# Twenty-four gate products of a merge as pairs by seven half-size products, with the sums of their weights made in DRAM

## What is computed

```python
gates = jax.nn.sigmoid(p["gate"] + merge_gate_b).reshape(Bn, S, N_BRANCH, D_MODEL)
merged = (gates[:, :, 0] * y_ml + gates[:, :, 1] * y_gla
          + gates[:, :, 2] * y_conf + gates[:, :, 3] * y_sc)
return merged @ w_o
```

## Time and profile before

| what | value |
| --- | --- |
| median of 3 runs | 1973.35 us (1972.5 to 1974.92) |
| the profiled execution | 1973.15 us, span 1971.2 us |
| granted PE clock, mean | 0.999 of full speed |
| PE, DVE, ACT, POOL busy | 1959.5, 1291.6, 893.8, 128.4 us |
| merge loop, one output tile | 27.2 us |

### The profile page before, as it was taken

One profiled execution on the slowest core, in us unless ns is written; L12 is line 12 of the kernel. 1 busy time (PEld: TensorE's weight loads), 2 busy tenths in 40 slices (PEclk: granted clock), 3 DMA queues, 4 the chain that ended last, 5 costly groups with the idle time before them and its releaser, 6 DMA issues.

```text
span 1971.2 us, 29262 instructions
## 1 busy us (share of the span) xinstructions
PE 1959.5 (99%) x10404; PEld 1640.5 (83%) x10404; DVE 1291.6 (66%) x2073; ACT 893.8 (45%) x1417; POOL 128.4 (7%) x202
## 2 busy tenths in 40 slices
PE   9999999999999999999999999999999999999999
PEld 7777789898987888898998888778888888888888
DVE  6555578676687776787786679484444786653545
ACT  4555555445444554544454443564333544432333
POOL 0111011111111111000001000000000000000000
PEclk9999999999999999999999999999999999999999
DMA  5899968677666115666656313111322412232222
GB/s 200 211 232 240 203 180 204 198 188 189 221 209 150 55 50 149 199 177 186 191 178 244 110 44 106 64 65 66 106 96 96 144 43 86 95 100 103 93 93 91
DMA packets 92909, 278.80 MB, mean 141 GB/s; under 512 B 10488, under 2 KB 13560, under 8 KB 92560
## 3 DMA queue, kind: packets, MB, share of 16 engines
q1 hardware_dynamic: 67200, 187.20, 29.1%
q0 software_dynamic: 24896, 88.14, 18.8%
q10 hardware_dynamic: 720, 2.23, 0.3%
HBM read 275.39 MB, written 52.47 MB: 166 GB/s over the span
## 4 chain that ended last, share of the span: by engine, by line
PE 95%; DVE 2%; DMA 1%; ACT 1%; issue 0%; SPq 0%; DVEq 0%; ACTq 0%
PE bank L962 23%; PE bank L964 23%; PE bank L963 23%; PE bank L1285 4%; PE bank L1287 4%; PE bank L1286 4%; PE bank L1085 1%; DMA w_raw<-in_wstream 1%; PE bank L1144 1%; PE bank L1067 1%; PE bank L1160 1%; PE bank L1070 1%; PE bank L1018 1%; PE bank L1112 1%; PE bank L1020 1%; PE bank L1019 1%
## 5 line engine op out<-in xcount | busy, mean ns | idle before, releaser
L962 PE MATMUL bank<-b_hi,w_hi 128*128 128x512 f32 x2060 | 812.3, 394 | 2.7 <-DVE w_lo L3172 1.3
L964 PE MATMUL bank<-b_hi,w_lo 128*128 128x512 f32 x2060 | 802.2, 389 | 0.0
L963 PE MATMUL bank<-b_lo,w_hi 128*128 128x512 f32 x2060 | 802.0, 389 | 0.0
L962 PEld LDWEIGHTS bank<-b_hi,w_hi 128*128 128x128 f32 x2060 | 386.8, 188 | 91.1 <-issue 8.4
L964 PEld LDWEIGHTS bank<-b_hi,w_lo 128*128 128x128 f32 x2060 | 386.8, 188 | 81.1
L963 PEld LDWEIGHTS bank<-b_lo,w_hi 128*128 128x128 f32 x2060 | 387.0, 188 | 80.2 <-issue 2.4
L2835 DVE TENSOR_TENSOR w_lo<-w_raw,w_hi 128x1024 fp32r<-128x1024 f32 (+3 forms) x259 | 306.7, 1184 | 216.9 <-ACT w_hi L1879 216.0
L1879 ACT ACTIVATE w_hi<-w_raw 128x1024 fp32r<-128x1024 f32 (+3 forms) x259 | 265.6, 1025 | 285.0 <-PE bank L964 265.6
L3995 DVE SCALAR_TENSOR_TENSOR arena<-bank,vec,arena 128x511 f32<-128x511 f32 x88 | 65.7, 749 | 85.9 <-ACT arena L2729 80.6
L1285 PE MATMUL bank<-parts,w_hi 128*128 128x256 f32 x384 | 108.1, 282 | 0.1
L1287 PE MATMUL bank<-parts,w_lo 128*128 128x256 f32 x384 | 108.0, 281 | 0.0
(11 more groups left out here) (403 smaller groups left out, 2550.0 us busy)
## 6 DMA issues: line engine op xcount, KB each, us to landing
w_raw<-in_wstream SPq DMA_DIRECT2D x253, 512.0 KB, 3.5
arena<-in_ada POOLq DMA_DIRECT2D x30, 512.0 KB, 4.6
plain<-seven_sums SPq DMA_DIRECT2D x48, 256.0 KB, 5.0
early<-seven_sums SPq DMA_DIRECT2D x48, 256.0 KB, 4.2
plain<-in_wseven SPq DMA_DIRECT2D x36, 256.0 KB, 4.7
early<-in_wseven SPq DMA_DIRECT2D x36, 256.0 KB, 5.3
plain<-in_ada POOLq DMA_DIRECT2D x18, 512.0 KB, 4.4
seven_sums<-in_wseven POOLq DMA_DIRECT2D x16, 512.0 KB, 5.2
```

What stands on the lines that cost most here:

```text
L962: nc.tensor.matmul(dst, whi, rhs_hi(k), start=(k == 0), stop=False)
L963: nc.tensor.matmul(dst, whi, rhs_lo(k), start=False, stop=False)
L964: last = nc.tensor.matmul(dst, wlo, rhs_hi(k), start=False, stop=(k == n - 1))
```

## The change

The 24 gates of j = 2 to 7 are taken in pairs (12 units, 2 for each j), each by seven products of 12 matmuls of 128x256. The other 8 gates stay as they were.

- **Weights.** `gate_parts` makes four sums for each unit in DRAM: six serial DMAs on POOL for each j, each over the 2 units of that j (256 rows). Those of j = 2 to 6 are 30 DMAs, those of j = 7 are 6.
- **Activations.** `whole(k)`, k = 0 to 3, puts high plus low of two slices of h back together: a copying DMA from `b_hi` and an accumulating one from `b_lo`, both on POOL, each waited for. DVE's `gate_sums(k)` (4 operations of 128x256) makes the sums, ACT their high and DVE their low part (128x1024 each). `whole(2)` waits for `gate_sums(0)`, `whole(3)` for `gate_sums(1)`.
- **Ring.** Weights come as groups of two (one 128x512 piece each) into a ring of four buffers of 512 KB; the branch panel of j is one group of it. ACT and DVE split by pieces of 128x512.
- **Reading.** A product's bank is no longer read by the sigmoid alone. Of a unit's seven products DVE reads 0, 1 and 2 by writing a gate's half (`gate_set`, 128x256), then 3, 4 and 5 by adding to it (`gate_add`), ACT reads 6 with the sigmoid of one half (`last_gate_set`), and two more ACT operations make the other sigmoids in place (`gates_out`). Within a unit products 0, 2, 4 and 6 accumulate in one bank: product 2 waits for the read of 0, product 4 for that of 2, product 6 for that of 4.
- The loops over j are unrolled on all engines.

Core of the diff, POOL:

```diff
+            pool.wait_ge(h_lo, KT)
+            whole(0)
+            whole(1)
+            gate_parts(2, 7)
             pool.wait_ge(head_h, 2)
             for w in gla_w:
                 pool.memset(w, 0.0).then_inc(pads_set, 1)
+            whole(2)
+            whole(3)
+            gate_parts(7, KT)
```

```diff
+            def whole(k):
+
+                to = gate_whole[:, 2 * (k % 2):2 * (k % 2) + 2, :]
+                src = [b[0][:, 2 * k:2 * k + 2, :].bitcast(F32) for b in (b_hi, b_lo)]
+                if k >= 2:
+                    pool.wait_ge(mix_set, MIXED0 + 2 * UNITS + k - 1)
+                pool.dma_start(to, src[0]).then_inc(whole_in, 16)
+                pool.wait_ge(whole_in, next(landed))
+                pool.dma_start(to, src[1], accum_op=ALU.add).then_inc(whole_in, 16)
+                pool.wait_ge(whole_in, next(landed))
+
+            def gate_parts(j0, j1):
+                for j in range(j0, j1):
+                    for part in range(6):
+                        sum_part(2 * UNITS + unit(j, 0), GATE_U, part)
```

PE, the products and what they wait for:

```diff
+            def gate_products(j, u):
...
+                pe.wait_ge(seven_lo, item_count(j, item(u)))
+                if n == 0 and o == 0:
+                    pe.wait_ge(gate_done, 2 * BRANCHES)
+                if n == 0 and o == 1:
+                    pe.wait_ge(mixed_low, MIXED_LOW0 + 2 * UNITS + QUAD)
+
+                before = {0: (n - 2, 6), 1: (n - 1, 5), 2: (n, 0), 3: (n - 1, 3), 4: (n, 2), 5: (n, 1), 6: (n, 4)}[o]
+                if before[0] >= 0:
+                    pe.wait_ge(*seen(*before))
...
+            for j in range(2, KT):
+                for u in range(GATE_U * SEVEN):
+                    gate_products(j, u)
+                    if u == KT - 1:
+                        pe.wait_ge(seven_lo, item_count(j, BRANCH_ITEM))
+                        branch_tiles(j - 1, 1)
```

DVE, the loop (each `gate_low` is 128x512, that of BRANCH_ITEM 128x1024):

```diff
+            dve.wait_ge(head_lo, 4)
+            gate_sums(2)
+            gate_low(2, 0)
+            gate_low(2, 1)
+            gate_sums(3)
+            gate_sums_low(2)
+            gate_sums_low(3)
+            branches(0, 0, lambda: (gate_low(2, 2), gate_low(2, 3)))
+            for j in range(2, KT):
...
+                gate_set(j, 7)
+                gate_low(j, 10)
+                branches(j - 1, (j - 1) % 2, lambda: (gate_low(j, 11), gate_low(j, 12)))
+                gate_set(j, 8)
+                gate_low(j, 13)
+                gate_set(j, 9)
+                gate_low(j, 14)
```

More of the change, by code:

```diff
@@ L782, in _, with load_rest @@
             base += (MIX0 - PANEL0["mla_out"]) * P * PANEL
[L783 to L787, removed]
+            def load_rest(first, last, at):
+                with sp.Fori(0, (last - first) // 2) as half:
+                    for s in range(2):
+                        load(s, 2 * half + (first + s), (2 * half + s) * (P * PANEL) + at, PANEL)
+                return at + (last - first) * P * PANEL
@@ new lines, in _ @@
+            merge = PANEL0["merge"]
+            base = load_rest(MIX0, merge + KT, base)
+            load(0, merge + KT, base, PANEL)
+            for j in range(2, KT):
+                sp.wait_ge(sum_in, gate_sums_made(j))
+                for q in range(KT):
+                    load_gates(j, q)
+            sp.wait_ge(seven_lo, item_count(KT - 1, BRANCH_ITEM))
+            load(1, merge + KT + 1, base + P * PANEL, PANEL)
+            sp.wait_ge(seven_lo, item_count(KT - 1, item(11)))
+            last = N_PANELS - KT
@@ L788, in _ @@
+            base = load_rest(merge + KT + 2, last, base + 2 * P * PANEL)
             width = FFN2_CHUNKS[-1] * P
@@ L2611, in _ @@
                 act.activation(early_gate[n], early_gate[n], ACT.Sigmoid).then_inc(gate_done, 1)
[L2614 to L2623, removed]
+                if n == EARLY - 4:
+                    gate_sums_high(2)
+            for n in range(EARLY - 2, EARLY):
+                act.wait_ge(mm_done, t0 + n + 1)
+                act.activation(early_gate[n], s_bank[n % 2][:], ACT.Sigmoid,
+                               bias=col("gate_b", n % BRANCHES * KT + n // BRANCHES)).then_inc(gate_done, 1)
             def merged_high(j, m):
@@ L3835, in branches @@
                     if b == 2:
-                        if not (isinstance(j, int) and j < 2):
+                        if j >= 2:
                             dve.wait_ge(merge_hi, j - 1)
@@ new lines, in gate_add @@
+            def gate_add(j, u):
+                e, h, bank, op, set_ = ((0, 0, s_bank[2], ALU.add, 0), (1, 1, s_bank[u // SEVEN], ALU.subtract, 1),
+                                        (0, 1, t_bank[0], ALU.add, 2))[u % SEVEN - 3]
+                dve.wait_ge(seven_mm, products_done(j, u))
+                dve.wait_ge(*seen(unit(j, u // SEVEN), set_))
+                to = gate[j % 2][2 * (u // SEVEN) + e][:, HALVES[h]]
+                dve.tensor_tensor(to, to, bank[:, 0:T // 2], op).then_inc(seven_read, 1)
@@ L3879, in w_o_split @@
             def w_o_split(j):
                 split((PANEL0["w_o"] + j) // 2, j % 2)
-            branches(KT - 2, 0)
             w_o_split(0)
```

324 lines of the change are left out of this document (245 added, 79 removed).

## The result

| | median us | range, runs | profiled span | PE clock |
| --- | --- | --- | --- | --- |
| before | 1972.92 | 1970.95 to 1974.92, 4 | 1971.2 | 0.999 |
| after | 2041.04 | 2037.82 to 2044.42, 4 | 2042.6 | 0.982 |

The change makes the kernel slower: the ratio is 1.0345, 95% interval 1.0325 to 1.0366, or 68.1 us by the medians. The forecast was 2012 us with a range to 2045: right in direction and mechanism, 29 us short in size, and 4 us inside the upper end.

What follows compares the result with a forecast made beforehand. The prediction took PE, busy 99% of the span, to bound the kernel. Its terms: 1973.15 - 11.3 + 30.2 + 1.5 + 12.2 + 6.2 + 0.3 = 2012.3, stated as 2012 us, range 1978 to 2045.

Steps and rivals of the forecast that it cites:

- PE work: FFN merge loop: seven products of 128x256 matmuls per pair, 9.94 us instead of 10.88; twelve pairs save 11.3 us.
- The memsets behind the sums: POOL's queue before GLA: memsets of gla_w stand behind 30 serial DMAs, delaying masked and chunk_states; PE idles 30.2 us.
- I take 6.5: POOL's sums of weights: assumed us per serial part of two units, between estimates of 5.9 and 6.9.
- The bound of 8.13: POOL's sums: upper bound in us per part, from one accumulating 512 KB DMA; PE would idle 77 us.
- PE restarts: After PE's long idle time before GLA's states: low granted clock costs 1.5 us, with ends 0 and 3.
- The late halves: Merge start: whole(2) and whole(3) land late; product 1 waits 7.6 us, product 2 4.6 more, together 12.2 us.
- Waits inside a tile: Merge loop: DVE's order delays product 11 by 0.77 and product 13 by 0.26 us; six tiles lose 6.2 us.
- The end: Behind the merge loop: the last branch panel's low part comes 0.3 to 0.6 us late; 0.3 taken.
- Being in time: Rival, POOL before GLA: parts cost 5.4 us or less, masked is on time, 1980.6 us; chance 0.15.
- The ring: Rival, weight loads in the merge loop: 48 groups each 0.8 us late add 38 us, 2050 us; chance 0.07.
- no change: Rival, POOL's DMAs under about 3.5 us each, with a start wait of 3 to 8 us: 1970 to 1977; chance 0.05.
- faster: Rival, POOL's DMAs under about 3.5 us each: sums done by 1270, kernel at 1962 to 1968 us; chance 0.10.

Runs made afterwards that it cites:

- the first experiment: Against the kernel after, the two memsets on POOL stand behind 18 of the 30 parts: 1981.71 us.
- two more edits and a third: Beside memsets behind 18 parts: VectorE's tile order changed, then whole(2) and whole(3) as VectorE adds, 1971.85 us; third, the merge's start reordered, 1965.1 us.
- four edits: Against the kernel after: memsets behind 18 parts, VectorE's tile order, whole(2) and whole(3) on VectorE, the merge's start reordered: 1965.1 us.

## Why the prediction was right, and where its sizes were off

- **PE work, 11.3 us.** 10.8: an undisturbed tile is 25.4 us against the 25.3 worked out.
- **The memsets behind the sums, 30.2 us: the mis-sized term.** The chain (POOL's 30 parts, its memsets, `masked`, `chunk_states`) was as described, but the wait is 60.7 us. The step that failed is "I take 6.5" for a part, which took 7.74: 29 x 1.24 = 36.0 us too little. Two choices made it so, and a third number eased it. The size step of 1.35 us was read from loads of 64 and 512 KB; doubling the units in a part really cost 7.74 - 5.41 = 2.3 us. And I went below 6.9 because the stretch had a DMA share of only 0.23, but that share is one without the sums: with them it is 0.74. Half-size parts there take 5.41, as good as the 5.59 of the FFN. In the forecast's own terms: 6.5 + 0.4 (not going below 6.9) + 1.0 (the step) - 0.2 (5.41 for 5.59) = 7.7. Against this, `whole(0)` and `whole(1)` cost 16.2 us and not 22: 5.8 back. 30.2 + 36.0 - 5.8 = 60.4. The bound of 8.13, set by the one accumulating DMA of that size, held 7.74 and was nearer than what I took; it did not quite stand alone, since POOL issued a load of 512 KB 0.56 us after it, and the DMA share was 0.87. That 2041 fell inside the range is partly luck: without the 5.8 us that `whole` gave back it would have been 2047, past the 2045.
- **The rule weighed against it.** A part of 512 KB took 6 to 10 us here, one of 1 MB 7 to 8. The Trainium skill's page DMA: Bandwidth & Descriptors (Anatomy of one DMA, SWDGE path), has a fit (2.0 us plus the bytes at 436 GB/s); the estimates worked out from it are 3.2 and 4.4 us, and 0.8 us for a unit's mean of 341 KB, where the runs with two and ten units show 1.96. For such DRAM-to-DRAM sums this trace disagrees with it, and the case that it led to, sums done by 1270, did not come.
- **PE restarts, 1.5 us.** 2.6 behind the long wait, and about 2.5 behind the waits at the merge's start, which the forecast had not counted. No row of before had such a wait, and the end of 3 was about the long one alone. The dip of 0.93 in before, taken as the pattern for the restart, is a loss of before itself: by the rows above 1.3 us of it do not come again, which no term of the forecast holds.
- **The late halves, 12.2 us.** 8.6 us before product 1 (for 7.6; the DMAs of the two late pairs took 23.2 us, not 22) and 3.0 before product 2 (for 4.6): 11.6.
- **Waits inside a tile, 6.2 us.** The tile is 26.35 where 26.3 was worked out. Product 11 is 0.66 late (0.77), product 13 0.15 (0.26). The read from PSUM without a row took 0.42 us, as taken.
- **The end, 0.3 us.** 0.43.
- **The rivals.** Being in time (1980.6) did not come by itself, but the first experiment made that case: 1981.7. The ring did not starve: from 1464 to 1613 us PE has no wait but those before product 11 and the short gaps before product 13, and they end with DVE. The mechanism of "no change" and "faster", DMAs of under 3.5 us, did not come at all; the times were reached in another way, after two more edits and a third.

## What to carry to other kernels

When work is added to an engine's queue, look at what stands behind it and who wants that, not at the engine's busy share: POOL is 8% busy here and cost 60 us, because its two memsets, 1.3 us, stood behind 241 us of DMAs (1146.51 to 1387.71), each waited for. Price a serial DMA by the row nearest in kind and size (DRAM to DRAM, accumulating, the same bytes), and read the load on the queues as it will be with the new transfers, not as it was; where transfers must be serial, few large ones were cheaper here than many small ones (141 us for six, 232 for 30, about 325 for 60). A saving on the bound engine shows only when each wait round it is gone: here the 7.7 us came out after four edits, three of which changed nothing but order.

## What the runs showed of the hardware that I had not expected

- Serial sums of weights in DRAM by GpSimd's DMAs, issue to issue: 5.41 us for one unit, 7.74 for two, 23.45 for ten (a unit is 512 KB in the two copying parts and 256 KB in the four accumulating ones).
- A DMA share of 0.71 over 156 us beside the kernel's own loads delayed nothing there: `masked` started at 1326.87, in before at 1327.07. With the DMAs of ten units (share 0.79 over the 156 us) PE lost 1.1 us and `masked` started at 1328.24.
- Waits of PE of 8.7 and 3.0 us, not only long ones, were followed by a low granted clock (0.75 to 0.79 over 6 us), and a wait of 4.3 us by 0.84 over 6; behind one of 2.5 us the matmuls started 0.12 us apart, as at 1.00, and with waits of 1.2 us and less it was 1.00 over the stretch. But a low clock does not need a wait: in before it was 0.72 from 1340 to 1346 us with PE busy throughout. After 155.3 us of idle time it was 0.77 over the first 7 us and then 1.00, so a long wait costs no more at the restart than one of 17.7 us (0.69 over 6 us).
